# One 512-column product in place of two 256-column products in the feed-forward blocks of a two-model kernel

## What is computed

```python
def swiglu(h, w_gate, w_up, w_down):
    return (jax.nn.silu(h @ w_gate) * (h @ w_up)) @ w_down

h = h + swiglu(rms_norm(h, ln_ffn[layer]), e_ffn_w_gate[j], e_ffn_w_up[j], e_ffn_w_down[j])   # once, 1024 -> 2816 -> 1024
...
x = x + 0.5 * swiglu_ffn(h, ffn1_w_gate[l], ffn1_w_up[l], ffn1_w_down[l])                     # l = 0, 1
...
x = x + 0.5 * swiglu_ffn(h, ffn2_w_gate[l], ffn2_w_up[l], ffn2_w_down[l])                     # l = 0, 1
```

## Time and profile before

| | |
|---|---|
| median of three runs | 2889.73 us (2888.15 to 2890.3) |
| span of the profiled execution, first to last instruction | 2887.0 us |
| its mean granted TensorE clock | 0.946 of 2.4 GHz |
| TensorE matmul busy | 2600.4 us, 90% |
| TensorE weight load busy | 2204.6 us, 76% |
| VectorE busy | 1777.1 us, 62% |
| ScalarE busy | 1242.4 us, 43% |
| products of 256 columns in the feed-forward blocks | 3 x 1760 |
| moved by DMA | 601.34 MB, mean 208 GB/s |

### The profile page before, as it was taken

One profiled execution on the slowest core, in us unless ns is written; L12 is line 12 of the kernel. 1 busy time (PEld: TensorE's weight loads), 2 busy tenths in 40 slices (PEclk: granted clock), 3 DMA queues, 4 the chain that ended last, 5 costly groups with the idle time before them and its releaser, 6 DMA issues.

```text
span 2887.0 us, 36005 instructions
## 1 busy us (share of the span) xinstructions
PE 2600.4 (90%) x14026; PEld 2204.6 (76%) x14026; DVE 1777.1 (62%) x1749; ACT 1242.4 (43%) x1026; POOL 59.6 (2%) x35
## 2 busy tenths in 40 slices
PE   8699897677999999999999997998789989986997
PEld 6399785565778787878778786997569979964996
DVE  4455344443889898988888896553735445453553
ACT  2333201212667676767666675332133343311432
POOL 0000001210000000000000000000100000001000
PEclk9899998887999999999999998999899999998998
DMA  8255142002989898989999898552326565430453
GB/s 322 78 186 174 58 146 88 1 1 88 337 315 364 302 372 307 357 318 348 330 336 337 313 371 313 184 196 67 106 83 200 184 226 175 144 129 17 161 195 102
DMA packets 313146, 601.34 MB, mean 208 GB/s; under 512 B 6017, under 2 KB 130049, under 8 KB 312833
## 3 DMA queue, kind: packets, MB, share of 16 engines
q1 hardware_dynamic: 313088, 600.55, 58.7%
HBM read 599.48 MB, written 1.05 MB: 208 GB/s over the span
## 4 chain that ended last, share of the span: by engine, by line
PE 64%; DVE 7%; PEld 3%; DVEq 2%; issue 2%; ACT 2%; DMA 1%; PEldq 0%; ACTq 0%
PE bank L172 18%; PE bank L174 18%; PE bank L173 18%; PE bank L383 3%; PE bank L1757 2%; DVE scratch L1896 2%; DVE weights_lo L1665 2%; PE bank L1442 1%; DVEq L1897 1%; PE bank L1492 1%; PEld bank L174 1%; PEld bank L172 1%; PEld bank L173 1%; PE bank L1466 1%; DMA scratch<-in_ffn_w_gate 1%
## 5 line engine op out<-in xcount | busy, mean ns | idle before, releaser
L1665 DVE TENSOR_TENSOR weights_lo<-mslot,weights_hi 128x2048 fp32r<-128x2048 f32 x338 | 769.6, 2288 | 89.5 <-ACT weights_hi L1544 84.2
L1544 ACT ACTIVATE weights_hi<-mslot 128x2048 fp32r<-128x2048 f32 x338 | 646.4, 1918 | 256.2 <-PE bank L174 183.8
L481 DVE TENSOR_TENSOR weights_lo<-scratch,weights_hi 128x2048 fp32r<-128x2048 f32 x165 | 377.3, 2291 | 410.2 <-ACT weights_hi L474 407.4
L172 PE MATMUL bank<-x_hi,weights_hi 128*128 128x256 f32 x1760 | 504.6, 287 | 28.1 <-DVE x_lo L308 19.2
L173 PE MATMUL bank<-x_lo,weights_hi 128*128 128x256 f32 x1760 | 503.6, 286 | 0.0
L174 PE MATMUL bank<-x_hi,weights_lo 128*128 128x256 f32 x1760 | 503.4, 286 | 0.0
L474 ACT ACTIVATE weights_hi<-scratch 128x2048 fp32r<-128x2048 f32 x165 | 316.1, 1921 | 346.2 <-PE bank L174 304.0
L172 PE MATMUL bank<-weights_hi,x_hi 128*128 128x512 f32 x904 | 371.5, 411 | 32.6 <-DVE weights_lo L1665 32.6
L172 PEld LDWEIGHTS bank<-x_hi,weights_hi 128*128 128x128 f32 x1760 | 343.8, 195 | 31.9 <-DVE x_lo L308 20.9
L174 PE MATMUL bank<-weights_hi,x_lo 128*128 128x512 f32 x904 | 360.7, 399 | 0.0
L173 PE MATMUL bank<-weights_lo,x_hi 128*128 128x512 f32 x904 | 360.6, 399 | 0.0
(11 more groups left out here) (340 smaller groups left out, 2317.9 us busy)
## 6 DMA issues: line engine op xcount, KB each, us to landing
mslot<-in_o_moe_w_down SPq DMA_DIRECT2D x58, 2048.0 KB, 8.6
mslot<-in_o_moe_w_gate SPq DMA_DIRECT2D x57, 2048.0 KB, 8.9
mslot<-in_o_moe_w_up SPq DMA_DIRECT2D x57, 2048.0 KB, 9.0
scratch<-in_ffn_w_gate SPq DMA_DIRECT2D x44, 1024.0 KB, 7.1
scratch<-in_ffn_w_up SPq DMA_DIRECT2D x44, 1024.0 KB, 5.5
scratch<-in_ffn_w_down SPq DMA_DIRECT2D x44, 1024.0 KB, 5.0
mslot<-in_o_w_in SPq DMA_DIRECT2D x8, 2048.0 KB, 8.4
mslot<-in_w_in SPq DMA_DIRECT2D x10, 1536.0 KB, 10.0
```

Of the source, the lines that this page charges most:

```text
L172: pe.matmul(out, stationary[0], moving[0], start=start, stop=False)
L481: dve.tensor_tensor(m.wlo[i][:, :], m.fslot[i], m.whi[i][:, :], ALU.subtract).then_inc(m.sig["f_lo"], 1)
L1544: act.activation(m.whi[places[half]][:, :], raw[:, half * PIECE:(half + 1) * PIECE], ACT.Copy).then_inc(s["r_hi"], 1)
L1665: dve.tensor_tensor(m.wlo[places[half]][:, :], raw[:, half * PIECE:(half + 1) * PIECE], m.whi[places[half]][:, :], ALU.subtract).then_inc( ...
```

## The change

The tokens' parts become one tensor `m.x2` of 8 x 2 x 256, so that the high and low part of one step lie side by side, and one product of 512 columns with the weights' high part takes both. It writes a whole bank: the first 256 columns are high by high, the last 256 are high (weights) by low (tokens). The product with the weights' low part stays, of 256 columns, and adds to the first half. So each half j has a bank of its own (banks 0 and 1 for gate, 2 and 3 for up), and the two halves of a bank have still to be added: ScalarE copies the low half into `m.xT`'s space (`low_part`), and VectorE adds the other half to it, for gate and for up, 128 x 256 each. silu and the multiplication then read that sum from SBUF. `f_gdone` and `f_udone` now count halves, and `f_gsum`, `f_usum` say that the banks are free.

```diff
-    m.xh, m.xl = cut(sb("x_hi", KT * SEQ, F32R), 0, KT, SEQ), cut(sb("x_lo", KT * SEQ, F32R), 0, KT, SEQ)
+    m.x2 = cut(sb("x_parts", KT * 2 * SEQ, F32R), 0, KT, 2, SEQ)
+    m.xh, m.xl = m.x2[:, :, 0, :], m.x2[:, :, 1, :]
...
         for j in range(FU // P):
             cols = slice(j * P, (j + 1) * P)
             for k in range(KT):
-                last = split_product(pe, m.ps[bank][:, j * SEQ:(j + 1) * SEQ], (hi[:, k, cols], lo[:, k, cols]),
-                                     (m.xh[:, k, :], m.xl[:, k, :]), start=(k == 0), stop=(k == KT - 1))
-        last.then_inc(s[done], 1)
+                both = m.x2[:, k].rearrange("p i t -> p (i t)")
+                pe.matmul(m.ps[bank + j][:, :], hi[:, k, cols], both, start=(k == 0), stop=False)
+                last = pe.matmul(m.ps[bank + j][:, 0:SEQ], lo[:, k, cols], m.xh[:, k, :],
+                                 start=False, stop=(k == KT - 1))
+            last.then_inc(s[done], 1)
...
-            pe.wait_ge(s["f_silu"], u + at)
+            pe.wait_ge(s["f_gsum"], 2 * (u + at))
         inner("gate", 0, "f_gdone")
...
-            pe.wait_ge(s["f_h"], u + at)
-        inner("up", 1, "f_udone")
+            pe.wait_ge(s["f_usum"], 2 * (u + at))
+        inner("up", 2, "f_udone")
...
+    def low_part(u, done, bank, free, out, copied):
+        if not (v == 0 and isinstance(u, int) and u == 0):
+            act.wait_ge(s[free], u + at)
+        for j, cols in enumerate(halves):
+            act.wait_ge(s[done], 2 * (u + at) + j + 1)
+            act.activation(out[:, cols], m.ps[bank + j][:, SEQ:2 * SEQ], ACT.Copy).then_inc(s[copied], 1)
+
+    def gate(u):
+        low_part(u, "f_gdone", 0, "f_silu", f.glow, "f_gcopy")
+
+    def silu(u):
+        act.wait_ge(s["f_gsum"], 2 * (u + at) + 2)
         if not (v == 0 and isinstance(u, int) and u == 0):
             act.wait_ge(s["f_h"], u + at)
-        act.activation(silu, m.ps[0][:, :], ACT.Silu).then_inc(s["f_silu"], 1)
+        act.activation(f.silu, f.glow, ACT.Silu).then_inc(s["f_silu"], 1)
+
+    def up(u):
+        low_part(u, "f_udone", 2, "f_h", f.ulow, "f_ucopy")
...
     with act.Fori(1, NU - 1) as u:
-        one(u)
+        gate(u)
+        silu(u)
         ffn_hi(act, m, v, "gate", u + 1)
         ffn_hi(act, m, v, "down", u)
+        up(u)
         ffn_hi(act, m, v, "up", u + 1)
...
+    def gate(u):
+        for j, cols in enumerate(halves):
+            dve.wait_ge(s["f_gcopy"], 2 * (u + at) + j + 1)
+            dve.tensor_tensor(f.glow[:, cols], m.ps[j][:, 0:SEQ], f.glow[:, cols], ALU.add).then_inc(s["f_gsum"], 1)
 
     def hidden(u):
-        dve.wait_ge(s["f_udone"], u + at + 1)
+        for j, cols in enumerate(halves):
+            dve.wait_ge(s["f_ucopy"], 2 * (u + at) + j + 1)
+            dve.tensor_tensor(f.ulow[:, cols], m.ps[2 + j][:, 0:SEQ], f.ulow[:, cols], ALU.add)
+        dve.drain().then_inc(s["f_usum"], 2)
         dve.wait_ge(s["f_silu"], u + at + 1)
-        dve.tensor_tensor(h, m.ps[1][:, :], silu, ALU.mult)
+        dve.tensor_tensor(f.h, f.ulow, f.silu, ALU.mult)
```

More of the change, by code:

```diff
@@ L466, in ffn_parts_free @@
     if not (v == 0 and isinstance(u, int) and u == 0):
-        eng.wait_ge(m.sig[f"f_{kind[0]}done"], u + v * NU)
+        eng.wait_ge(m.sig[f"f_{kind[0]}done"], (u + v * NU) * (1 if kind == "down" else 2))
 def ffn_hi(act, m, v, kind, u):
@@ L485, in ffn_act @@
     s, at = m.sig, v * NU
-    silu = ffn_silu(m)
-    def one(u):
-        act.wait_ge(s["f_gdone"], u + at + 1)
+    f = ffn_hidden(m)
+    halves = [slice(j * SEQ, (j + 1) * SEQ) for j in range(FU // P)]
+    def low_part(u, done, bank, free, out, copied):
[4 more added lines that the diff above has]
+            act.activation(out[:, cols], m.ps[bank + j][:, SEQ:2 * SEQ], ACT.Copy).then_inc(s[copied], 1)
@@ L490, in one @@
+    def gate(u):
+        low_part(u, "f_gdone", 0, "f_silu", f.glow, "f_gcopy")
+    def silu(u):
+        act.wait_ge(s["f_gsum"], 2 * (u + at) + 2)
         if not (v == 0 and isinstance(u, int) and u == 0):
             act.wait_ge(s["f_h"], u + at)
-        act.activation(silu, m.ps[0][:, :], ACT.Silu).then_inc(s["f_silu"], 1)
-    one(0)
+        act.activation(f.silu, f.glow, ACT.Silu).then_inc(s["f_silu"], 1)
+    def up(u):
+        low_part(u, "f_udone", 2, "f_h", f.ulow, "f_ucopy")
+    gate(0)
@@ L495, in ffn_act @@
+    silu(0)
     ffn_hi(act, m, v, "gate", 1)
     ffn_hi(act, m, v, "down", 0)
+    up(0)
     ffn_hi(act, m, v, "up", 1)
     with act.Fori(1, NU - 1) as u:
-        one(u)
+        gate(u)
+        silu(u)
         ffn_hi(act, m, v, "gate", u + 1)
         ffn_hi(act, m, v, "down", u)
+        up(u)
         ffn_hi(act, m, v, "up", u + 1)
-    one(NU - 1)
+    gate(NU - 1)
+    silu(NU - 1)
     ffn_hi(act, m, v, "down", NU - 1)
-def ffn_silu(m):
-    return m.xT.rearrange("p k t -> p (k t)")[:, 0:HALF]
+    up(NU - 1)
@@ L511, in ffn_dve, with ffn_hidden @@
+def ffn_hidden(m):
+    f, flat = Place(), m.xT.rearrange("p k t -> p (k t)")
+    f.silu, f.h, f.glow = (flat[:, i * HALF:(i + 1) * HALF] for i in range(3))
+    f.ulow = flat[:, 3 * HALF:4 * HALF]
+    return f
 def ffn_dve(dve, m, v, scale):
     s, at = m.sig, v * NU
-    silu, h = ffn_silu(m), m.xT.rearrange("p k t -> p (k t)")[:, HALF:2 * HALF]
+    f = ffn_hidden(m)
+    halves = [slice(j * SEQ, (j + 1) * SEQ) for j in range(FU // P)]
+    def gate(u):
+        for j, cols in enumerate(halves):
+            dve.wait_ge(s["f_gcopy"], 2 * (u + at) + j + 1)
+            dve.tensor_tensor(f.glow[:, cols], m.ps[j][:, 0:SEQ], f.glow[:, cols], ALU.add).then_inc(s["f_gsum"], 1)
@@ L521, in hidden @@
             dve.wait_ge(s["f_ddone"], u + at)
-        dve.tensor_copy(m.hh[:, :], h)
+        dve.tensor_copy(m.hh[:, :], f.h)
         dve.drain()
-        dve.tensor_tensor(m.hl[:, :], h, m.hh[:, :], ALU.subtract).then_inc(s["f_h"], 1)
+        dve.tensor_tensor(m.hl[:, :], f.h, m.hh[:, :], ALU.subtract).then_inc(s["f_h"], 1)
+    gate(0)
     ffn_lo(dve, m, v, "gate", 1)
@@ L1318, in moe_mem @@
     flat = lambda t: t.rearrange("p k t -> p (k t)")
-    r.xgh, r.xgl = (flat(t)[:, 0:KT * P].rearrange("p (k t) -> p k t", k=KT) for t in (m.xh, m.xl))
-    free_1, free_2 = 6 * PIECE + KT * P, 6 * PIECE + KT * SEQ + KT * P
+    x2 = m.x2.rearrange("p k i t -> p (k i t)")
+    r.xgh, r.xgl = (x2[:, i * KT * P:(i + 1) * KT * P].rearrange("p (k t) -> p k t", k=KT) for i in range(2))
+    free_1, free_2 = 6 * PIECE + 2 * KT * P, 6 * PIECE + 3 * KT * P
     r.y = m.scr(free_1, D)
```

## The result

Ten runs of the changed kernel on one chip, among ten of the kernel before:

| | median | lowest to highest |
|---|---|---|
| before | 2888.0 us | 2883.7 to 2890.7 |
| changed | 2893.0 us | 2891.1 to 2897.1 |

The account below looks back on a forecast made before the run. TensorE's own stream was taken as the bound inside the blocks. Savings of 22.2 us less losses of 4.5, 5.0 and 2.4 gave 10.3 us off the 2887.0 span, 2876.7; with the median 2.7 above, 2879.4 us, range 2869 to 2893.

Parts of the forecast that it names:

- What bounds the kernel: Inside the feed-forward blocks TensorE's own stream is the bound; TensorE is busy for 90% of the span.
- The cost of a product in a uniform stream: On TensorE, 256 columns cost 120 ns and 512 cost 226.5 ns, about 13.5 ns of each independent of width.
- The step of the mixed stream: Gate and up on TensorE: a step falls from 360 to 347 ns, 22.2 us saved over 1705 steps.
- The sum: The forecast's addition for the whole kernel: 22.2 - 4.5 - 5.0 - 2.4 = 10.3 us saved.
- rival (a): Gate and up: a wide product next to a narrow one is dearer; 2901.6 us, or 2893.1 at 240 + 115; chance 0.12.
- the point that the prediction named for the turning: Gate and up: the change stops paying where a step saves less than 11.9 / 1705 = 7 ns.
- Its own sign of being wrong: A gate or up step not between 337 and 355 ns, or the clock falling inside the loop.
- Unit 0: First unit of a block: gate(1) waits 1.1 us for its split piece in four blocks, 4.5 us lost.
- The pause ahead of down(10): Last unit: copy, semaphore, addition and drain lengthen the 2.14 us pause by 1.0 us in five blocks, 5.0 us lost.
- The clock behind it: During down(10): half clock after 3.5 of five pauses instead of 2, 1.6 us each, 2.4 us lost, bounds 0 and 4.8.
- The loop's cover: Inside the loop: a unit's four copies and four additions cost nothing, hidden values having 2.5 us spare; loads start as before.

## Why the prediction was wrong

- **What bounds the kernel**: right. TensorE's stream is the bound in the loop, and with all added work but three products the unit stayed at 16.98 us.
- **The cost of a product in a uniform stream**, 120 and 226.5 ns: right, also for the new moving operand.
- **The step of the mixed stream failed.** The sum took 226.5 + 120 = 347 ns, a saving of 13, arguing that the two departures at a change of width are opposite and cancel. They are opposite, but in strict alternation the wide product costs 10 ns more and the narrow one gives back only 3: 353 ns. The saving is 7 ns a step, and 10.3 us in all instead of 22.2 by the unit times. The rows of the kernel before held a hint: the 24 products of down behind the narrow ones take 5.47 us in the earlier trace rows, 0.03 more than 24 x 226.5 ns, and nothing as large comes back on the narrow side. This is rival (a) in its milder case, 240 + 115 = 355 ns a step and 2893.1 us; the whole of (a) had 0.12. That the time fits it to 0.1 us is partly luck, since its other losses were the 11.9 of the sum and not the 15.3 measured. 7 ns is the point that the prediction named for the turning, with losses of 11.9. Its own sign of being wrong, a step outside 337 to 355 ns, did not show; those bounds let in steps at which the change no longer pays. The formula of the Trainium skill ("TensorE: Matmul & The Clock Gate", section "Back-to-back issue gap") gives an estimate of 325.0 ns a step and 2.5 ns saved; the trace has 353 and 7. Its saving is nearer than my 13 all the same, which is chance, for its cost of a step is 28 ns off and mine 6.
- **Unit 0**: right in mechanism and place (copy, table load, silu, split), 0.95 us in four blocks where 1.1 were forecast, and covered by the DMA in the second. With the second block's wait, 0.3 shorter, that is 3.5 lost where the sum had 4.5 (4 x 1.1 is 4.4). That the clock would not fall behind this pause was right.
- **The pause ahead of down(10)**: right, 3.1 us and 4.8 lost where 5.0 were forecast.
- **The clock behind it was mis-sized.** The sum took 3.5 falls of 1.6 us instead of 2, 2.4 more, with 4.8 as the bound. In this profile it fell behind all five, where three or four were forecast, and two lost 2.7 us: 7.0 more. Both falls in the rows cost 1.6 and I took that for the most that one can cost.
- **The loop's cover** (VectorE's and ScalarE's added work, the loads): right, it cost nothing.

The two failed terms are 22.2 - 10.3 = 11.9 and 7.0 - 2.4 = 4.6 us. The waits give 1.2 back, which leaves the 15.3 between 10.3 saved and the ledger's 5.0 lost. The first alone turns the forecast saving of 10.3 into a loss of 1.6; the second alone would have left 5.7 saved.

## What to carry to other kernels

Replacing two narrow products by a wide one saves only the fixed part of a product (13 ns of 120 here), so weigh that against every microsecond that the extra work of getting its result out of the banks adds where nothing covers it: the first unit, the last one. Read the cost of a product in the very order in which it will run, since a uniform stream does not tell it, and try wide and narrow ones in pairs. The exposed last unit was worth more than the whole change: half-by-half hand-over took 14.8 us off the kernel before.

## What was not expected of the hardware

Alternating products of 512 and 256 columns take 353 ns a pair, 7 more than the sum of what each costs among its like (226.5 and 120). In the order two and two most of that is gone: 348 ns, and units of 16.59 us against 16.79. And a pause of TensorE of about 3.1 us was followed by half clock in 34 of 40 cases (the eight profiles that have it, five blocks each, told by the time from down(10)'s first product to the block's end: 8.2 us at full clock, 9.6 to 11.1 otherwise), against 2 of 5 after 2.1 us, none of 28 after the 0.8 to 1.0 us ahead of gate(1) (the seven profiles that have it, four blocks each), and none of 10 after 0.6 to 0.7 ahead of down(10).
